# Seven products of a 2x2x2 partition in place of the eight blocks of one output product, with weight sums made two stages earlier

## The reference

```python
x = x + jnp.concatenate([ret, dsa], axis=-1) @ w_out[i]
gate = jax.nn.sigmoid(rms_norm(x, norm_ple[i]) @ w_ple_gate[i])
x = x + gate * (p[i] @ w_ple_proj[i])
...
return rms_norm(x, norm_final)
```

## Time and profile before

| | us |
|---|---|
| median of three runs | 2103.07 |
| lowest, highest | 2099.49, 2103.81 |
| the profiled execution | 2101.14 |
| its span in the profile | 2099.2 |
| TensorE busy in the span | 1984.0 (95%) |
| VectorE busy | 1456.5 (69%) |
| ScalarE busy | 782.0 (37%) |
| GpSimd busy | 514.4 (25%) |
| mean granted clock of TensorE, share of full | 0.976 |

### The profile page before, as it was taken

One profiled execution on the slowest core, in us unless ns is written; L12 is line 12 of the kernel. 1 busy time (PEld: TensorE's weight loads), 2 busy tenths in 40 slices (PEclk: granted clock), 3 DMA queues, 4 the chain that ended last, 5 costly groups with the idle time before them and its releaser, 6 DMA issues. The chain is left out here.

```text
span 2099.2 us, 27565 instructions
## 1 busy us (share of the span) xinstructions
PE 1984.0 (95%) x10153; PEld 1482.2 (71%) x10153; DVE 1456.5 (69%) x2486; ACT 782.0 (37%) x1571; POOL 514.4 (25%) x556
## 2 busy tenths in 40 slices
PE   6999999998998999999999997899999888989998
PEld 3854474567876888888888887757888655668775
DVE  6673596548998557777567696589999788651423
ACT  2222111237144333333344444464121446751425
POOL 1910000134310003333000013225667352200210
PEclk9999999999999999999999998999999999999999
DMA  8443111113242235565464442112111110031101
GB/s 331 172 125 126 50 41 40 31 47 135 81 131 71 90 126 166 190 202 174 148 203 145 141 155 97 57 51 77 50 50 35 30 61 21 1 134 48 41 0 81
DMA packets 143098, 207.59 MB, mean 99 GB/s; under 512 B 16414, under 2 KB 83294, under 8 KB 139642
## 3 DMA queue, kind: packets, MB, share of 16 engines
q1 hardware_dynamic: 136794, 184.92, 27.1%
q0 software_dynamic: 6080, 20.98, 2.6%
q10 hardware_dynamic: 96, 0.02, 0.0%
HBM read 169.90 MB, written 34.66 MB: 97 GB/s over the span
## 5 line engine op out<-in xcount | busy, mean ns | idle before, releaser
L3113 DVE TENSOR_SCALAR_CACHE_REDUCE pj_junk<-NM,prm 128x384 uint8<-128x384 f32 (+1 forms) x186 | 163.7, 942 | 1.1
L1759 PE MATMUL ps<-pj_part,h 128*128 128x512 f32 x384 | 153.2, 399 | 0.3 <-ACT PJ L2970 0.2
L1760 PE MATMUL ps<-pj_part,h 128*128 128x512 f32 x384 | 150.3, 391 | 0.0
L1761 PE MATMUL ps<-pj_part,h 128*128 128x512 f32 x384 | 150.2, 391 | 0.0
L3055 POOL TENSOR_TENSOR pj_part<-pj_raw,pj_part 128x512 fp32r<-128x512 f32 x64 | 84.7, 1326 | 157.6 <-ACT pj_part L2965 156.5
L1759 PE MATMUL ps<-w_end,se_hT 128*128 128x512 f32 x256 | 106.9, 418 | 0.4 <-DVE se_hT L3849 0.4
L1041 PE MATMUL ps<-mx_w,HT 128*128 128x272 f32 (+1 forms) x320 | 106.5, 493 | 0.0
L1761 PE MATMUL ps<-w_end,se_hT 128*128 128x512 f32 x256 | 99.9, 390 | 0.0
L1760 PE MATMUL ps<-w_end,se_hT 128*128 128x512 f32 x256 | 99.7, 389 | 0.0
L2965 ACT ACTIVATE pj_part<-pj_raw 128x512 fp32r<-128x512 f32 x64 | 40.6, 639 | 149.4 <-DMA pj_raw<-in_w_in 146.3
L1759 PEld LDWEIGHTS ps<-pj_part,h 128*128 128x128 f32 x384 | 72.4, 189 | 29.1 <-issue 14.1
(11 more groups left out here) (861 smaller groups left out, 5420.4 us busy)
## 6 DMA issues: line engine op xcount, KB each, us to landing
s_wm<-in_w_mod SPq DMA_DIRECT2D x16, 1024.0 KB, 4.6
pj_raw<-in_w_in SPq DMA_DIRECT2D x64, 256.0 KB, 2.6
ff_m<-in_w_ffn_out SPq DMA_DIRECT2D x44, 256.0 KB, 4.4
ff_sums<-ff_m SPq DMA_DIRECT2D x44, 256.0 KB, 4.3
mod_w<-in_w_mod SPq DMA_DIRECT2D x8, 1024.0 KB, 9.0
ff_w0p<-in_w_ffn_in SPq DMA_DIRECT2D x22, 256.0 KB, 3.2
ff_w1p<-in_w_ffn_in SPq DMA_DIRECT2D x22, 256.0 KB, 3.5
ff_hid<-ff_d POOLq DMA_DIRECT2D x20, 256.0 KB, 3.4
```

The lines of the kernel that those rows point to most:

```text
L1759: nc.tensor.matmul(out, w[0], x[0], start=first, stop=False)
L1760: nc.tensor.matmul(out, w[0], x[1], start=False, stop=False)
L1761: return nc.tensor.matmul(out, w[1], x[0], start=False, stop=last)
L3113: last = v.tensor_scalar(junk[:, packed(j + 2)], x, bound(j), 0.0, ALU.is_ge, ALU.add, accum_out=cnt[:, j:j + 1])
```

## The change

In stage_second_end rows, inner width and columns are halved each. A11, A12, A21, A22 are the quarters of the transposed mixed rows (row half, inner half), now evicted once as plain float32, one copy by ScalarE and one by VectorE per tile. VectorE makes S1 to S4 from them. The seven products come in the order 1, 2, 6, 5, 3, 7, 4, each with four inner tiles, a unit of 12 matmuls per inner tile over four banks. Products 6, 7 and 4 are accumulated onto what their banks already hold, product 3 onto product 5, and after every product VectorE adds the four banks into the quarter of x that needs this state of the sum. The rows of a step are split into four rotating pairs of tiles (steps), high by ScalarE, low by VectorE. Weights of the first four products are there from the attention stage; those of the last three are loaded, split by ScalarE and GpSimd during the stage. The first half of the rows is complete after the fifth product, so turns 0 and 1 stand behind its sixth product's last two units, and turns 2 and 3 behind the first two banks of the last product, which is made bank by bank.

Four of the seven weight operands are sums. They are made in the feed-forward's output product: at units 16, 23, 30, 37 SP loads four blocks of w_out_2, GpSimd makes a quartet of subtractions, and five units later SP stores four sums to K.sums_end.

The diff, cut to its core:

```diff
--- stage_join_ffn, SP, inside the loop over the loads of output units (q is the unit)
+                j = (q - 16) // 7
+                if q >= 16 and j < KH and (q - 16) % 7 == 0:
+                    if j:
+                        sp.wait_ge(end_st, end_base + 64 * j)
+                    for n, (k, c) in enumerate(((j, 0), (j, HALF), (KH + j, 0), (KH + j, HALF))):
+                        sp.dma_start(made_end[n][:], w_end[k][:, c:c + HALF]).then_inc(end_in, 16)
+                elif q >= 16 and j < KH and (q - 16) % 7 == 5:
+                    sp.wait_ge(end_sum, end_sum_base + 4 * j + 4)
+                    b11, b12, b21, b22 = made_end
+                    for p, t in ((4, b21), (5, b11), (6, b22), (7, b12)):
+                        sp.dma_start(K.sums_end[p - 4, j], t[:]).then_inc(end_st, 16)
...
--- stage_join_ffn, GpSimd, ahead of the rows of x2
+            for j in range(KH):
+                pool.wait_ge(end_in, end_base + 64 * (j + 1))
+                g.tensor_tensor(b11[:], b12[:], b11[:], ALU.subtract).then_inc(end_sum, 1)
+                g.tensor_tensor(b12[:], b22[:], b12[:], ALU.subtract).then_inc(end_sum, 1)
+                pool.wait_ge(end_sum, end_sum_base + 4 * j + 2)
+                g.tensor_tensor(b22[:], b22[:], b11[:], ALU.subtract).then_inc(end_sum, 1)
+                pool.wait_ge(end_sum, end_sum_base + 4 * j + 3)
+                g.tensor_tensor(b21[:], b21[:], b22[:], ALU.subtract).then_inc(end_sum, 1)
...
--- attention stage, SP: the second half of the weights
-                sp.dma_start(K.raw_end[b][:], I["w_out_2"][0].rearrange("(k p) n -> p k n", p=P)[:, :, b * HALF:(b + 1) * HALF]).then_inc(w_in[b], 16)
+                    for m, p in enumerate((6, 5)):
+                        sp.dma_start(K.raw_end[b][:, 4 * m:4 * m + 4, :], K.sums_end[p - 4].rearrange("k p n -> p k n")).then_inc(w_in[b], 16)
...
--- stage_second_end
+    rows_in = {1: A11, 2: A12, 6: S2, 5: S1, 3: S4, 7: S3, 4: A22}
+    steps = [[K.at(f"se_st{n}{m}", 40 + 4 * n + 2 * m, [P, HALF], FR) for m in range(2)] for n in range(4)]
+    ORDER = (1, 2, 6, 5, 3, 7, 4)
+    into = {1: (0, 0), 2: (0, 0), 6: (0, 1), 5: (1, 1), 3: (0, 1), 7: (1, 1), 4: (1, 0)}
...
--- TensorE
-            for i in range(NT):
-                output(0, i)
-            for i in range(NT):
-                output(1, i)
-                if i >= 2:
-                    turn(i - 2)
+            def three(o, j, n):
+                p, u = ORDER[o], KH * o + j
+                bank = K.bank[n if p in (1, 6, 7, 4) else 4 + n]
+                xh, xl = (x[:, n * P:(n + 1) * P] for x in steps[u % 4])
+                wh, wl = step_parts(u)
+                for m, (x, y) in enumerate(((xh, wh), (xh, wl), (xl, wh))):
+                    mm = nc.tensor.matmul(bank[:], x, y, start=(j == 0 and m == 0 and p in (1, 2, 5)), stop=(j == KH - 1 and m == 2), skip_group_check=True)
+                return mm
...
+            for u in range(6 * KH):
+                unit(u)
+                if u >= 6 * KH - 2:
+                    turn(u - 6 * KH + 2)
+            for n in range(4):
+                last_bank(n)
+                if n < 2:
+                    turn(2 + n)
+            turn(4)
...
--- ScalarE
+            def step_high(u):
+                p, j = units[u]
+                if u >= 4:
+                    act.wait_ge(S["omm"], u - 3)
+                rows_wait(act, p, j)
+                nc.scalar.activation(steps[u % 4][0][:], rows_in[p][:, j, :], ACT.Copy).then_inc(S["xhi"], 1)
...
+            split(0, 4)
+            split(0, 5)
+            high(1)
+            size(2)
+            split(0, 6)
+            split(0, 7)
+            size(3)
...
--- VectorE
+            def sums(j):
+                v.tensor_tensor(S1[:, j, :], A21[:, j, :], A22[:, j, :], ALU.add).then_inc(S["s1"], 1)
+                v.tensor_tensor(S2[:, j, :], S1[:, j, :], A11[:, j, :], ALU.subtract).then_inc(S["s2"], 1)
+                v.tensor_tensor(S4[:, j, :], A12[:, j, :], S2[:, j, :], ALU.subtract).then_inc(S["s4"], 1)
...
+            for u in range(6 * KH + 3):
+                step_low(u)
+                if KH <= u < 2 * KH:
+                    sums(u - KH)
+                elif 2 * KH <= u < 3 * KH:
+                    third_sum(u - 2 * KH)
+                if u >= 6 and u % 4 == 2 and u < 6 * KH:
+                    for n in range(4):
+                        residual(u // 4 - 1, n)
...
+            residual(5, 0)
+            step_low(6 * KH + 3)
+            for n in range(1, 4):
+                residual(5, n)
+            low(0)
+            low(1)
+            scale(2, h[0][:], S["ssr"], ss, 0, S["hr"])
+            residual(6, 0)
+            scale(3, h[1][:], S["ssr"], ss, 0, S["hr"])
```

More of the change, by code:

```diff
@@ L3690, in stage_second_end @@
     x_in, g_in = [K.sem(f"se_xin{q}") for q in range(4)], [K.sem(f"se_gin{q}") for q in range(4)]
-    names = "mtr mhi mlo ptr ptev omm oev ssr hr htr hhi hlo ghi glo pmm gmm gr used x4 ssr2 outr chain".split()
+    x_w = [K.sem(f"se_xw{q}") for q in range(3)]
+    names = "mtr mea med s1 s2 s3 s4 xhi xlo whi wlo obk ptr ptev omm oev ssr hr htr hhi hlo ghi glo pmm gmm gr used x4 ssr2 outr chain".split()
     S = {n: K.sem("se_" + n) for n in names}
@@ L3725, in _ @@
         def _(pool):
+            for u in range(2 * KT, len(units)):
+                pool.wait_ge(S["whi"], u - 2 * KT + 1)
+                (s, at), (h, l) = w_tile[u], step_parts(u)
+                nc.gpsimd.tensor_tensor(l, K.raw_end[s][:, at, :], h.bitcast(F32), ALU.subtract).then_inc(S["wlo"], 1)
             for b in range(2):
@@ L3728, in _, with bank_free @@
                     pool.wait_ge(S["ghi"], KT * b + k + 1)
[L3729 removed]
+                    (s, at), (h, l) = g_tile[b][k], parts(b, k)
+                    nc.gpsimd.tensor_tensor(l, K.raw_end[s][:, at, :], h.bitcast(F32), ALU.subtract).then_inc(S["glo"], 1)
         @block.tensor
         def _(pe):
[L3733 to L3740 removed]
+            def bank_free(o, n):
+                if o == 0:
+                    pe.wait_ge(S["ptev"], 4)
+                elif o == 1:
+                    pe.wait_ge(S["mea"], NT)
+                    pe.wait_ge(S["med"], NT)
+                else:
+                    last = {2: 0, 3: 1, 4: 3, 5: 2, 6: 5}[o]
+                    pe.wait_ge(S["oev"], 4 * last + n + 1)
@@ new lines, in ready, with unit @@
+            def ready(u):
+                pe.wait_ge(S["xlo"], u + 1)
+                if u >= 2 * KT:
+                    pe.wait_ge(S["wlo"], u - 2 * KT + 1)
+            def unit(u):
+                o, j = u // KH, u % KH
+                ready(u)
+                for n in range(4):
+                    if j == 0:
+                        bank_free(o, n)
+                    mm = three(o, j, n)
+                    if j == KH - 1 and n < 3:
+                        mm.then_inc(S["obk"], 1)
+                mm.then_inc(S["omm"], 1)
@@ L3742, in turn, with last_bank @@
+            def last_bank(n):
+                bank_free(6, n)
+                for j in range(KH):
+                    if n == 0:
+                        ready(KH * 6 + j)
+                    mm = three(6, j, n)
+                mm.then_inc(S["omm"], 1)
             def turn(i):
@@ L3767, in gates @@
                         pe.wait_ge(S["glo"], KT * b + k + 1)
-                    last = product(nc, K.bank[6 + n % 2][:], [x[:, k, i * P:(i + 1) * P] for x in hT], [x[:, k, :] for x in w[b]],
+                    last = product(nc, K.bank[6 + n % 2][:], [x[:, k, i % NH * P:(i % NH + 1) * P] for x in hT[i // NH]], parts(b, k),
                                    k == 0, k == KT - 1)
@@ L3794, in _ @@
                 gates(0, i)
-                if i < 2:
-                    turn(NT - 2 + i)
+                if i < 3:
+                    turn(5 + i)
             for i in range(NT):
@@ L3853, in residual, with third_sum @@
+            def third_sum(j):
+                dve.wait_ge(S["xlo"], j + 1)
+                v.tensor_tensor(S3[:, j, :], A11[:, j, :], A21[:, j, :], ALU.subtract).then_inc(S["s3"], 1)
+            def residual(o, n):
+                half, b = into[ORDER[o]]
+                i, first = 4 * half + n, o in (0, 2, 3, 6)
                 x = x3(i)[:, b * HALF:(b + 1) * HALF]
-                if b == 0 and i % 2 == 0:
+                if first:
                     dve.wait_ge(x_in[i // 2], 16)
-                dve.wait_ge(S["omm"], n + 1)
```

200 lines of the change are left out of this document (143 added, 57 removed).

## The result

The changed kernel takes **2105.86 us** (median of 9 runs, 2103.71 to 2109.1) against 2100.39 for the kernel before beside it (9 runs); the ratio is **1.0026** with a 95% interval of [1.0016, 1.0036]. So the change costs 5.5 us: slower, and clear of the interval, where I had forecast -0.3 us, no change at 2102.8. The time lies inside my range, the cause is one that I had not named.

The account below looks back on a forecast made before the run. The prediction took TensorE's own stream as the bound in the last stage and feed-forward. Terms -10.9 + 0.4 + 4.1 + 1.7 + 4.4 = -0.3 us, from a median of 2103.07 to 2102.8 us; range 2096.5 to 2108.5.

Parts of the forecast that it names:

- The 48 matmuls: Last stage's output product: 336 matmuls instead of 384, at 0.227 us each, -10.9 us.
- The start: Start of the last stage: first product begins later, behind evictions and the first high and low halves, +0.4 us.
- The hand-over: Last stage, products to gates: turn 2 waits 3.9 us for VectorE's scaling, turns 3 and 4 do not; +4.1 us.
- The clock behind it: Last stage, after the stop at turn 2: TensorE's granted clock falls, +1.7 us.
- The seven products: Last stage: TensorE waits for no low half, bank or weight load within the products, 0 us.
- The weight sums: Feed-forward's output product: GpSimd's quartets delay VectorE, so TensorE stops 2.5 and 1.9 us, +4.4 us; the least trusted term.
- Both 0: Weight sums' transfers: SP's waits for stores, and loading two sums in the attention stage, each cost 0.
- Rival B: Feed-forward's output: VectorE becomes the bound, sums cost 11.1 us instead of 4.4; +6.4 us, 2109.5 us, chance 0.21.
- Rival A: Feed-forward: quartets hide where VectorE waits or reads PSUM, TensorE never stops; -4.7 us, 2098.4 us, chance 0.27.
- Rival C: Feed-forward: clock also falls behind two stops, 1.7 us each; +3.4 us, 2106.2 us, chance 0.10.

Follow-up runs that it names:

- the sums alone: Kernel before plus only the change's weight sums (GpSimd quartets, their loads and stores), attention and last stage as before: 2109.23 us, ratio 1.0036 to the kernel before.
- the last stage alone: Changed kernel without making weight sums, plain blocks of w_out_2 as operands instead: 2096.58 us, ratio 0.9984 to the kernel before.
- the queues apart: Changed kernel with the quartets' loads and stores issued on GpSimd's own queue instead of SP's: 2100.67 us, ratio 1.000 to the kernel before.
- the versions with calm places: Changed kernel, quartets moved to where VectorE pauses: 2098.3 us with transfers on GpSimd's queue; with two last-stage edits added 2091.34, and 2087.63 on SP's queue.

## Why the prediction was wrong, and where it was right

- **The 48 matmuls, -10.9: right, by the lengths.** The last stage is 228.5 us for 232.4. The terms as measured give -10.9 + 0.2 (start) + 3.5 (turn 2) + 3.4 (clock behind two stops) = -3.8 for the -3.9. From the first product to the first gate it is 88.1 for 92.7: -4.6, where the same terms with one turn fewer in that stretch (-0.9) give -4.9.
- **The start, +0.4: right in time, short in its follow-up.** The first product begins 13.0 us after the first transposes, 12.8 before: +0.2. But what had been two short waits with work between the earlier trace rows became one of 2.23, and behind it the clock fell for 1.7 us. That is why the stretch took 88 us and not 86. It is a fall that came in six of the seven kernels with this stop of 2.23 us, and stayed away in one.
- **The hand-over, +4.1: right.** 3.52 at turn 2 for 3.9, VectorE's queue in the order worked out, and turns 3 and 4 without a wait.
- **The clock behind it, +1.7: right,** 1.7. The trace of the changed kernel has the clock at 0.50 to 0.69 behind all four stops of 1.8 us or more, and at 0.43 and 0.80 us it stayed at 1.00. The Trainium skill (TensorE: Matmul & The Clock Gate, Part 1) has an idle TensorE fall to the lower rate, but not behind stops as short as 1.82 and 2.23 us; there the measurement decides.
- **The seven products, no wait: right.**
- **The weight sums, +4.4: wrong. This is the step that failed.** The runs give 7.5 (the sums alone) to 8.8 (the change against the last stage alone). Two of its sentences fell. "A quartet takes 4.4 us from VectorE" was read where GpSimd gets in the earlier trace rows and applied to the second quartet, in a stretch where VectorE is busy 19.84 us of 20; there VectorE loses nothing and GpSimd is held, 12.13 us in the changed kernel and 18.77 with the queues apart. And "SP waits for the stores ... Both 0" rested on a subtraction taking 1.3 to 1.7 us: held 12 us, it held SP, and SP the load for unit 29. For the first quartet the step held: it took 3.6 us from VectorE, and at unit 25 VectorE's lead was 1.4 us (split done at 1109.2, unit at 1110.6) for 3.9 before, some 2.4 less where I had worked out 2.0. The second quartet, which was to stop TensorE at that unit, then took nothing.
- **Rival B** gave 11.1 for the sums, a little nearer in size than my 4.4, but by VectorE becoming the bound; it was idle 8.25 us ahead of the stop. **Rival A** said that the sums hide at pauses and PSUM reads: that is what they do in the versions with calm places. **Rival C,** a clock fall behind two stops in the feed-forward, did happen, 3.3 us for its 3.4. That its 2106.2 us lies so near the 2105.86 measured is luck: the kernel before took 2100.39 beside it and not 2103.07, and the stops had another cause.
- The Trainium skill (GPSIMD Engine Reference, 8. Key points) puts the contention, among others, on VectorE instructions with two SBUF inputs. The trace agrees that PSUM reads let GpSimd run (1.29 us at 1105.28 beside them). Which of the two engines pays is what decided here, and for that this section has no rule: the trace shows both.

## What to carry to other kernels

When work moves to GpSimd beside VectorE, ask of the place not how busy VectorE is on average but whether it pauses. In these runs, with a pause GpSimd got in, and VectorE paid about 1.1 us for each of its operations beside a subtraction; in the unbroken run of SBUF operations from 1089 on, GpSimd was held to the run's end or to a PSUM read. A price read at one place, like that of the earlier trace rows, need not hold at another. Then ask who stands behind the held operation: an in-order queue that waits for it turns a free delay into a late load. And a stop of TensorE of 2 us or more is to be priced at the stop and some 1.7 us of slower clock behind it, also where it takes the place of two shorter ones; the price was 1.6 to 1.7 behind all four stops of the changed kernel, and nothing behind one stop of 2.23 us in another.

## What the hardware showed that I had not expected

- A GpSimd operation of 1.3 us (128x512, two SBUF inputs) can last 12.13 or 18.77 us beside VectorE's back-to-back operations of 0.68, none of which is longer for it; a copy of 0.61 us lasted 6.30. A pause of 0.42 us in VectorE was enough to end the one of 18.77.
- With the quartets' 32 transfers on GpSimd's queue, TensorE's wait for its own sequencer at the turn of ynT is 7.3 us (three kernels), with them on SP's queue 5.3 to 5.7 (seven kernels), without them 5.2 and 5.5. Why, no run tells.
